# Expert rows scaled at the eviction and added to a DRAM sum by a scatter for each item

## The reference

```python
def moe(x, ...):                       # x: 1024 tokens x 1024
    scores = sigmoid(x @ w_router)     # 64 experts
    idx = top_k(scores + router_bias, 8)
    gates = sel / sum(sel) * 2.5       # sel = scores[idx]
    # every token goes to its 8 experts, tokens of one expert in blocks of 128
    y = (silu(xb @ w_gate[e]) * (xb @ w_up[e])) @ w_down[e]   # hidden width 256
    routed = sum over the token's 8 experts of gate * y
    shared = (silu(x @ w_gate_sh) * (x @ w_up_sh)) @ w_down_sh
    return routed + shared
x = layer_norm(2**0.25 * x + moe(x), ln2_g, ln2_b)
```

## Time and profile before

| | |
|---|---|
| Median of 3 runs | 1631.55 us (1626.91 to 1634.21) |
| Profiled execution: its own time is its span | 1636.9 us |
| TensorE busy | 88% of the span |
| VectorE busy | 65% |
| ScalarE busy | 48% |
| GpSimd busy | 27% |
| DMA moved | 406.6 MB, 248 GB/s in the mean |
| Items, from the number of `y_d` writes | 103 |
| Mean granted TensorE clock | 0.920 |

### The profile page before, as it was taken

The page is one execution under the profiler, slowest core; times in us unless marked ns, Lnnn a source line. Parts: engine busy times, 40 slices in busy tenths (PEclk is TensorE's granted clock), DMA queues, the critical chain, the costliest instruction groups (busy, mean ns, idle before and its releaser), DMA issues.

```text
span 1636.9 us, 26706 instructions
## 1 busy us (share of the span) xinstructions
PE 1446.1 (88%) x6687; PEld 1173.5 (72%) x6688; DVE 1066.5 (65%) x1229; ACT 788.6 (48%) x1073; POOL 442.7 (27%) x419
## 2 busy tenths in 40 slices
PE   6969956699979999999998999999999979995664
PEld 5869835577767887888887888888878768883221
DVE  4497756367776685866785465476757856771766
ACT  3121145322133485865684566466757856761111
POOL 1066001126644221122222121122222212213562
PEclk9985986799879999999999999999999999997887
DMA  5112029867346388877897677777888987757995
GB/s 196 52 39 78 0 103 350 307 229 172 76 171 190 134 344 329 341 300 290 328 355 280 222 279 269 277 285 286 336 326 311 374 308 315 283 221 285 338 338 219
DMA packets 101489, 406.62 MB, mean 248 GB/s; under 512 B 19552, under 2 KB 19552, under 8 KB 75984
## 3 DMA queue, kind: packets, MB, share of 16 engines
q1 hardware_dynamic: 56848, 280.41, 46.3%
q0 software_dynamic: 29776, 71.77, 12.4%
q10 hardware_dynamic: 14832, 54.01, 8.2%
HBM read 327.10 MB, written 96.33 MB: 259 GB/s over the span
## 4 chain that ended last, share of the span: by engine, by line
PE 52%; DMA 18%; DVE 11%; issue 10%; POOL 5%; ACT 2%; POOLq 1%; DVEq 0%; ACTq 0%
PE ps L1507 23%; DMA idx<-list_d 14%; PE ps L1525 11%; PE ps L1326 5%; PE ps L1351 4%; DVE cv L936 3%; DMA xg<-x_d,idx 2%; PE ps L1362 2%; POOL yg L602 2%; POOL list_d L535 2%; PE ps L1439 1%; DMA xin<-in_x 1%; PE ps L1397 1%; DVE xres L1131 1%; PE ps L1426 1%
## 5 line engine op out<-in xcount | busy, mean ns | idle before, releaser
L1507 PE MATMUL ps<-wgu,xTe 128*128 (+1 forms) x2496 | 601.5, 397 | 7.9 <-issue 7.9
L1507 PEld LDWEIGHTS ps<-wgu,xTe 128*128 128x128 f32 x2496 | 466.6, 190 | 104.2 <-issue 10.9
L567 POOL DMA_INDIRECT xg<-x_d,idx x97 | 144.8, 1493 | 722.9 <-DMA idx<-list_d 435.9
L1525 PE MATMUL ps<-wdn,hT 128*128 (+1 forms) x1236 | 297.6, 390 | 1.3 <-DVE hT L1224 1.3
L1194 DVE TENSOR_TENSOR wgu<-raw,wgu (+1 forms) x130 | 292.1, 2289 | 1.9 <-issue 1.3
L1525 PEld LDWEIGHTS ps<-wdn,hT 128*128 128x128 f32 x1236 | 232.1, 188 | 49.7 <-DVE hT L1224 1.7
L728 ACT CAST wgu<-raw (+1 forms) x130 | 248.2, 1911 | 1.5 <-SPq L400 1.3
L1199 DVE TENSOR_TENSOR xTe<-ps,xTe 128x512 fp32r<-128x512 f32 x210 | 134.9, 684 | 125.3 <-ACT xTe L781 123.2
L1194 DVE TENSOR_TENSOR wdn<-raw,wdn (+1 forms) x65 | 149.0, 2293 | 71.7 <-ACT wdn L774 71.7
L786 ACT COPY ysb<-ps 128x512 f32<-128x512 f32 x206 | 110.8, 590 | 128.7 <-PE ps L1525 128.7
L774 ACT CAST wdn<-raw (+1 forms) x65 | 124.3, 1913 | 18.7 <-issue 18.7
(11 more groups left out here) (208 smaller groups left out, 1393.8 us busy)
## 6 DMA issues: line engine op xcount, KB each, us to landing
raw<-in_w_gate SPq DMA_DIRECT2D x64, 1024.0 KB, 7.2
raw<-in_w_up SPq DMA_DIRECT2D x64, 1024.0 KB, 9.8
raw<-in_w_down SPq DMA_DIRECT2D x64, 1024.0 KB, 8.4
y_d<-ysb ACTq DMA_DIRECT2D x103, 512.0 KB, 4.3
y_d<-zero SPq DMA_DIRECT2D x16, 2048.0 KB, 18.1
wraw<-in_w_in SPq DMA_DIRECT2D x10, 512.0 KB, 3.3
xin<-in_x POOLq DMA_DIRECT2D x8, 512.0 KB, 4.6
wraw<-in_w_kv SPq DMA_DIRECT2D x8, 512.0 KB, 3.2
```

The lines of the kernel that those rows point to most:

```text
L567: g.indirect_dma_start(out=xg[:, s], out_offset=None, in_=x1_d, in_offset=bass.IndirectOffsetOnAxis(ap=idx[:, s:s + 1], axis=0), bounds_ch ...
L1507: last = mm(ps[:, 2 + s, :], xTe[:, s, st, d], wgu[:, w, mo, d].rearrange("p a n -> p (a n)"), start=(d == 0 and st == 0 and mo == 0), sto ...
L1525: last = mm(ps[:, 5 + h, :], hT[:, s, st, c], wdn[:, w, mo, c, h * 512:(h + 1) * 512].rearrange("p a n -> p (a n)"), start=(c == 0 and st ...
```

## The change

- The list entries in `list_d` have two words, the token and its gate (divided by alpha, `tg`). Unused entries hold a token number from 1024 up, one of 128 spare rows, and gate 0. `scatter` writes both words.
- A DRAM tensor `acc_d` (1024 + 128 spare rows) takes the place of `y_d`. SyncE writes each x1 tile into it as well as into `x1_d`.
- ScalarE's eviction `y_out` scales by 1/alpha for the shared items and by the row's gate for the others, from a ring of 8 columns `gring`. It waits for the add of item i-4 (`s_add`) instead of the write, and issues no DMA.
- GpSimd copies each item's tokens and gates into the rings `iring` and `gring`, and issues for each item `add_rows`: an indirect DMA with an add, from `ysb` to the rows of `acc_d` that the tokens name. Each add waits until the one before has landed, since the same token may stand in both. The add of item i-4 is the last thing of `fetch(i)`; four are issued before the loop and three after it.
- The rows of `acc_d` then hold (alpha x1 + moe) / alpha, of which the layer norm is the same with its epsilon divided by alpha squared. In the tail SyncE loads eight tiles into eight buffers, then gain and shift, VectorE and GpSimd do the layer norm, SyncE stores. The gathers, the diagonals, TensorE's sums, `rows(t)`, `zero_rows` and the waits on them go.

```diff
@@ sync
-            for n in range(5):
-                zero_rows(n)
+            sp.dma_start(acc_d[S:TRASH, :], a["x"][0]).then_inc(s_trash, 16)
...
-                sp.dma_start(x1_d[t * 128:(t + 1) * 128, :], xres[:, t % 2]).then_inc(s_x1w[t % 2], 16)
-                if t < 3:
-                    zero_rows(5 + t)
+                for dst in (x1_d, acc_d):
+                    sp.dma_start(dst[t * 128:(t + 1) * 128, :], xres[:, t % 2]).then_inc(s_x1w[t % 2], 16)
...
-                    sp.wait_ge(s_x1w[t % 2], 16 * (t // 2 + 1))
+                    sp.wait_ge(s_x1w[t % 2], 32 * (t // 2 + 1))
...
             sp.wait_ge(s_endR, 4)
+            for t in range(NT):
+                sp.dma_start(acc[:, t], acc_d[t * 128:(t + 1) * 128, :]).then_inc(s_acc[t], 16)
             sp.dma_start(g2[:], a["ln2_g"].to_broadcast([128, D])).then_inc(s_g2, 16)
             sp.dma_start(b2[:], a["ln2_b"].to_broadcast([128, D])).then_inc(s_g2, 16)
             for t in range(NT):
                 sp.wait_ge(s_o, t + 1)
+                sp.dma_start(out[t * 128:(t + 1) * 128, :], acc[:, t]).then_inc(s_out[t % 2], 16)
@@ gpsimd
-                        in_=tok[:, t % 2:t % 2 + 1], in_offset=None,
+                        in_=tg[:, t, k], in_offset=None,
...
+            def add_rows(j, s):
+
+                g.wait_ge(s_y, 2 * j + 4)
+                if not isinstance(j, int) or j >= 1:
+                    g.wait_ge(s_add, 16 * j)
+                g.sem_inc(s_seen, 1)
+                slot = j % RING
+                g.tensor_copy(sidx[:, s:s + 1], iring[:, bass.ds(slot, 1)]).then_inc(s_sidx, 1)
+                g.wait_ge(s_sidx, j + 1)
+                g.sem_inc(s_seen, 1)
+                g.indirect_dma_start(
+                    out=acc_d, out_offset=bass.IndirectOffsetOnAxis(ap=sidx[:, s:s + 1], axis=0),
+                    in_=ysb[:, s], in_offset=None, compute_op=ALU.add,
+                    bounds_check=TRASH - 1, oob_is_err=True).then_inc(s_add, 16)
+
+            add_rows(0, 0)
+            add_rows(1, 1)
...
             def fetch(i, s, nth_next, nth):
 
                 gather(i + 1, 1 - s, nth_next)
                 load = token_list(i + 2, s)
+                slot = i % RING
+                g.tensor_copy(iring[:, bass.ds(slot, 1)], idx[:, s, 0:1]).then_inc(s_ring, 1)
+                g.tensor_copy(gring[:, bass.ds(slot, 1)], idx[:, s, 1:2].bitcast(F)).then_inc(s_ring, 1)
+                g.wait_ge(s_ring, 2 * (i - NT) + 2)
                 g.wait_ge(s_xg[s], 16 * nth)
                 g.sem_inc(s_seen, 1)
                 load()
-
+                add_rows(i - 4, s)
+
+            add_rows(2, 0)
+            add_rows(3, 1)
             token_list(NT, 0)()
             token_list(NT + 1, 1)()
             gather(NT, 0, 1)
...
+            before = g.value_load(nit[0:1, 1:2], min_val=NT + E - 3, max_val=MAX_ITEMS - 3)
+            g.wait_ge(s_y, 2 * n_items)
+            add_last((2 * (n_items // 2) + 6) % RING, 0, before)
+            add_last((2 * ((n_items + 1) // 2) + 5) % RING, 1, before + 1)
+            g.wait_ge(s_y, 2 * n_items + 2)
+            add_last((n_items + 7) % RING, 0, before + 2)
+            g.wait_ge(s_add, 16 * n_items)
+
             g.wait_ge(s_et, n_items + 2)
             g.sem_inc(s_endR, 1)
 
             g.wait_ge(s_endR, 4)
             for t in range(NT):
+                g.wait_ge(s_var, t + 1)
+                g.tensor_tensor(lnmv[:, t, 1:2], lnmv[:, t, 1:2], neghalf[:, 0:1], ALU.pow).then_inc(s_rstd, 1)
@@ scalar
+            def y_out(slot, scale):
                 for b in range(2):
-                    nc.scalar.copy(ysb[:, slot, b * 512:(b + 1) * 512], ps[:, 5 + b, :]).then_inc(s_y, 1)
+                    nc.scalar.activation(ysb[:, slot, b * 512:(b + 1) * 512], ps[:, 5 + b, :], ACT.Copy,
+                                         scale=scale).then_inc(s_y, 1)
...
+                if not shared or i >= 4:
+                    act.wait_ge(s_add, 16 * (i - 3))
                 if not shared or i >= 2:
-
-                    act.wait_ge(s_yd[s], 16 * nth)
                     act.wait_ge(s_dn, i - 1)
-                    y_out(s)
+                    y_out(s, 1.0 / ALPHA if shared else gring[:, bass.ds((i - 2) % RING, 1)])
                 item_hi(i + 1, 1 - s)
...
-                if not shared or i >= 2:
-                    act.wait_ge(s_y, 2 * i)
-                    act.dma_start(y_d[bass.ds((i - 2) * 128, 128), :], ysb[:, s]).then_inc(s_yd[s], 16)
...
+            before = act.value_load(nit[0:1, 1:2], min_val=NT + E - 3, max_val=MAX_ITEMS - 3)
+            act.wait_ge(s_add, 16 * before + 32)
             act.wait_ge(s_dn, n_items)
+            y_out(0, gring[:, bass.ds((n_items + 7) % RING, 1)])
             act.sem_inc(s_endR, 1)
@@ vector
+            def variance(t):
+                v.wait_ge(s_acc[t], 16)
+                for b in range(2):
+                    step(V.bn_stats(lnst[:, t, b], acc[:, t, b * 512:(b + 1) * 512]))
+                settle()
+                step(V.bn_aggr(lnmv[:, t], lnst[:, t].rearrange("p a b -> p (a b)")))
+                settle()
+                V.tensor_scalar(lnmv[:, t, 1:2], lnmv[:, t, 1:2], EPS / ALPHA ** 2, None, ALU.add).then_inc(s_var, 1)
+
+            variance(0)
+            v.wait_ge(s_g2, 32)
             for t in range(NT):
+                if t + 1 < NT:
+                    variance(t + 1)
+                v.wait_ge(s_rstd, t + 1)
+                step(V.scalar_tensor_tensor(acc[:, t], acc[:, t], lnmv[:, t, 0:1], g2[:], ALU.subtract, ALU.mult))
+                settle()
+                V.scalar_tensor_tensor(acc[:, t], acc[:, t], lnmv[:, t, 1:2], b2[:], ALU.mult,
+                                       ALU.add).then_inc(s_o, 1)
```

More of the change, by code:

```diff
@@ L87, in build @@
         mtmp = at("mtmp", 124, [128, ND, M])
-        zero = at("zero", 201, [128, 512])
+        fillw = at("fillw", 201, [128, 128, 2], U32)
+        tg = at("tg", 202, [128, NT, K, 2], U32)
         mst = at("mst", 136, [128, 2, 2, 8, 128], R)
@@ L272, in build @@
         s_y = sem("s_y")
-        s_yd = (sem("s_yd0"), sem("s_yd1"))
-        s_ylast = sem("s_ylast")
+        s_add = sem("s_add")
+        s_ring = sem("s_ring")
+        s_sidx = sem("s_sidx")
         s_endR = sem("s_endR")
-        s_cl = (sem("s_cl0"), sem("s_cl1"))
         s_g2 = sem("s_g2")
[L279 to L283, removed]
+        s_acc = [sem(f"s_acc{t}") for t in range(NT)]
+        s_var = sem("s_var")
+        s_rstd = sem("s_rstd")
         s_o = sem("s_o")
@@ L549, in _ @@
                     scatter(t - 2)
+            g.wait_ge(s_trash, 16)
+            for s in range(2):
+                g.wait_ge(s_x1w[s], 32 * 4)
+            def add_rows(j, s):
[13 more added lines that the diff above has]
+            add_rows(1, 1)
             for s in range(2):
                 g.wait_ge(s_sc[s], 16 * K * 4)
-            for s in range(2):
-                g.wait_ge(s_x1w[s], 16 * 4)
             g.wait_ge(s_tabs, 1)
@@ L1060, in rank @@
                 settle()
-                if u >= 2:
-                    v.wait_ge(s_sc[u % 2], 16 * K * (u // 2))
-                step(V.tensor_scalar(addr[:, u % 2], addrf[:], float(S), None, ALU.add))
-                step(V.tensor_scalar(tok[:, u % 2:u % 2 + 1], tokf[:, 0:1], float(128 * u), None, ALU.add))
+                step(V.tensor_scalar(addr[:, u], addrf[:], float(S), None, ALU.add))
                 settle()
@@ L1188, in item_tables_out @@
                 step(V.tensor_copy(nit[0:1, 0:1], endE[0:1, NE - 1:NE]))
+                step(V.tensor_scalar(nit[0:1, 1:2], endE[0:1, NE - 1:NE], -3.0, None, ALU.add))
                 settle()
@@ L1238, in step_v @@
                         gate_up_lo(nxt, 1)
-            def rows(t):
-                step(V.tensor_tensor(oh[:], iotaE[:].unsqueeze(1).to_broadcast([128, K, E]),
-                                     idxf[:, t].unsqueeze(2).to_broadcast([128, K, E]), ALU.is_equal))
-                settle()
-                step(V.tensor_tensor(ohx[:], oh[:], startE[:, 1:NE].unsqueeze(1).to_broadcast([128, K, E]), ALU.mult))
-                settle()
-                step(V.tensor_reduce(sel[:], ohx[:], AX.X, ALU.add))
-                settle()
-                step(V.scalar_tensor_tensor(yrow[:, t], sel[:], 128.0, rankK[:, t], ALU.mult, ALU.add))
             item_lo(0, 0)
```

184 lines of the change are left out of this document (46 added, 138 removed).

## The result

The changed kernel takes 1718.6 us (1714.8 to 1727.7), against 1634.2 us of the kernel before on the same chip: a ratio of 1.052 (95% interval 1.047 to 1.057), slower. The profiled execution has a span of 1726.1 us, against 1636.9.

What follows compares the result with a forecast made beforehand. The prediction saw TensorE's expert matmuls as a third of the span, late list loads in four stretches, and DMA 78% busy in the loop. 1636.9 - 98 + 5 + 43 + 12 = 1599 us, 1594 on the median; range 1530 to 1700.

Steps and rivals of the forecast that it cites:

- Tail, -98 us: Behind the item loop: loads, layer norm and stores take 53 us in place of 151, so 98 us less.
- Zero fill, second writes, VectorE's tables at nothing: Dropped 32 MB zero fill, SyncE's second tile writes and VectorE's row tables of shared items: each costed at nothing.
- Seams, +5 us: Loop's start and end: four early adds just fit, 0; the last adds delay the release by 5 us.
- Price of an add, 2.6 us of the engines: Item loop: an adding scatter of 512 KB costs two transfers' DMA work, 2.6 us, against 1.3 for a write.
- Crowded stretches, +43: Loop stretches with single-item experts: period grows from 12.3 to 13.6 us on 33 items, 43 us more.
- ScalarE, +12: ScalarE's new wait for the add of item i-4: 3 us once at each of four stretches, 12 us.
- Calm steps, +0: Calm stretches of the item loop: steps stay 9.29 us, since 18.6 us pass between eviction and need.
- that cycle (7.9 us): GpSimd's calm cycle: gather 1.0, list load 0.6, landing 6.0, gaps 0.3, in sum 7.9 us.
- 1.4 us of slack: GpSimd's calm cycle of 7.9 us against the 9.29 us step; two small copies use most of the slack.
- The prediction's own signs of being wrong: Calm steps over 9.5 us with GpSimd waiting; ScalarE waiting for adds in many steps; over 3.5 us engine time per add.
- The rival of a list load that is late everywhere: GpSimd's queue: adds delay the next list load, 128 us more, 1667 on the median; chance 0.17.
- The slow add: Item loop: an add costs 5.2 us of DMA work, 224 us more, 1763 on the median; chance 0.12.

Runs made afterwards that it cites:

- writes_nocopy: Changed kernel with ScalarE's plain writes for the adds and without GpSimd's two ring copies; sum over experts and gates left out: 1518.8 us, ratio 0.930.
- ahead_gates: Changed kernel with GpSimd's loop rewritten: eight-slot list ring read directly, no small copies, lists loaded three items ahead, one sum: 1579.0 us, ratio 0.974.
- before_ahead: Kernel before the change with its token lists in a ring of four slots and loaded three items ahead: 1605.8 us, ratio 0.989.

## Why the prediction was wrong

The forecast was 1594 us and the range ended at 1700; it took 1718.6. The profiled execution took 127 us more than the sum of 1599. By the terms of that sum:

- *Tail, -98 us.* Right: -101 (50 us left). VectorE does the first statistics and then waits for gain and shift, as said, 15.5 us after the release (its timeline in the changed kernel):

```profile
1691.38 1.29 DVE L1258 BATCH_NORM_STATS2 lnst<-acc 128x6 f32<-128x512 f32 x2 [10.08 <-DMA b<-in_ln_b]
```

- *Zero fill, second writes, VectorE's tables at nothing.* Not tried alone, and one run speaks against it. writes_nocopy has the loop of the kernel before but for these, and the new tail; 1635.7 less 101 would be 1535 us, and it takes 1518.8. Its 16 slow steps take 10.0 us in the mean, not 11.4. Whether the zero fill, the tables, the longer list entries or chance made this, no run tells.
- *Seams, +5 us.* At the end +13: from the last down matmul (1658.7) 17 us pass until the release, before the change 4. The adds there land after 6.3 us (1669.55 to 1675.86), with little else under way, where I had taken the write's 2.6 to 4. At the start the first list load comes at 545.7, 24 us later, not 12, for the same reason: the four adds before it are issued at 515.4, 524.4, 537.3 and 544.6. That put the steps of the loop 10 us back, where I had 0.
- *Price of an add, 2.6 us of the engines.* Nearly right in size: 2.9. That it is made of two transfers' work is argued, not shown.
- *Crowded stretches, +43, and ScalarE, +12.* In the changed kernel not borne out as worked: I had 33 steps of 13.6 us, but only 16 steps were slow before, and they went from 11.4 to 12.2, 13 us in all. With the list out of the way the size is there: the 96 steps of ahead_gates take 56 us more than those of before_ahead, all in 32 of them. That it comes to the 55 forecast is in part luck, since the two kernels are not those of the forecast.
- *Calm steps, +0.* Here the prediction failed. "In calm stretches two steps pass between eviction and need, 18.6 us, and it costs nothing" looks at one add's latency. But each add also waits for the one before, in the queue that issues the gathers and list loads, so the queue's cycle counts: 10.9 us against 9.29. I wrote out that cycle (7.9 us) and left the add out of it, saying that its copy and issue lie in the time of the list's landing. Its wait doesn't, and with a landing of 9.4 us the add's own cycle alone passes the step. And I priced the copies at 0.56 us each, "1.4 us of slack", where a copy and the step to the DMA that reads it took 1.1 us alone and 2.7 us beside VectorE. Together with the stalls that follow on ScalarE, the 96 steps grew by 167 us where the forecast had 55, all of it but 13 us in steps that took 9.29 before; with 10 us more at the start and 8 at the end that is the 130 by which the loop passed the forecast. The tail gave 3 back.

The prediction's own signs of being wrong came: calm steps over 9.5 us, GpSimd waiting for the previous add, and ScalarE's eviction waiting for an add in 69 steps.

The rival of a list load that is late everywhere, at 1667, had the right place, GpSimd's cycle, and the right point from which it decides, but named the wrong wait as the last: in the changed kernel it is the add (213 us on GpSimd, 411 on ScalarE), and the list comes second. Its price fell short for the same missing term, and it counted the two copies as 0.6 us together where the paragraph before it has 0.56 each. The slow add (1763) is out too: 2.9 us of the engines, not 5.2.

One more thing shows only when the runs are put side by side: the costs don't add. Moving one copy gives 61 us, taking the add operation away 116, a second sum 49, a new queue 140. That fits the reading that each shortens the same cycle until the next one rules. And it bounds what is shown: a short queue gives most of the loss back, and so does a plain scatter in the long queue (release 1676 to 1545). The loss is that of the two together, an add that lands late and a queue in which all else stands behind it.

## What to carry to other kernels

When an operation with a completion wait is put into a queue, write out one whole period of that queue, waits included, and compare it with the step; latency hidden for a single item says nothing about a chain in which each waits for the last. Where such a queue also issues the loads at the head of the pipeline, load further ahead and keep small copies out of it before touching the bytes. And measure a change against the kernel before with the same repair: here that control took half of the gain.

## What the runs showed of the hardware

- An adding scatter of 512 KB landed 5.9 us after its issue at the shortest in 940 to 1300 us (median 8.3 in ahead_gates, 9.4 in the changed kernel), a plain write of the same size by ScalarE in 2.6. It took 2.9 us of the 16 engines against 1.3 for a plain scatter, and GpSimd 1.61 us to issue against 1.03 for the plain scatter.
- A copy of one word per partition on GpSimd takes 0.18 us, and 1.81 us at 1210.06 in the timeline above. VectorE was in this operation then (timeline of VectorE in the changed kernel):

```profile
1209.54 4.49 DVE L1178 TENSOR_TENSOR wgu<-raw,wgu  x2
```

The Trainium skill (SBUF — State Buffer, § SBUF: two separate sides) has it that VectorE and GpSimd share a pair of ports, which one of them holds for a whole instruction, a VectorE operation with two SBUF inputs among them when GpSimd reads SBUF. The trace agrees: the copy ends at 1211.87, just after the second of the two VectorE operations has begun (1211.74), and VectorE was idle at 1202.44 and 1226.59, where the copy took 0.18 us.
- The add's issue that waits for such a copy starts 0.9 us after the copy's end, whether the copy took 0.18 or 1.81 us; the list load behind the ring copies starts 0.8 us after them.
